# Sums of squares per head in the forgetting attention's projections: two products of fp32r parts in place of one fp32 product

## The reference, cut to what matters

```python
h = rms_norm(x, mix_norm[i])
fq, fk, fv, f_logit, sq, sk, sv, g_fox, g_sb = split_columns(h @ w_in[i])
fq = rms_norm(fq.reshape(b, s_len, FOX_HEADS, HEAD_DIM), q_norm[i])
fk = rms_norm(fk.reshape(b, s_len, FOX_HEADS, HEAD_DIM), k_norm[i])
fv = fv.reshape(b, s_len, FOX_HEADS, HEAD_DIM)
log_f = jax.nn.log_sigmoid((f_logit + forget_bias[i]).astype(jnp.float32))
y_fox = forgetting_attention(fq, fk, fv, log_f)
```

## Time and profile before

| what | us |
|---|---|
| median of three runs | 1746.71 (1746.61 to 1747.81) |
| the profiled execution's own time | 1746.88 |
| its span | 1745.0 |
| PE busy in it | 1724.5 (99%) |
| VectorE busy | 1045.9 (60%) |
| ScalarE busy | 636.7 (36%) |
| POOL busy | 723.5 (41%) |

### The profile page before, as it was taken

The page is one execution under the profiler, slowest core; times in us unless marked ns, Lnnn a source line. Parts: engine busy times, 40 slices in busy tenths (PEclk is TensorE's granted clock), DMA queues, the critical chain, the costliest instruction groups (busy, mean ns, idle before and its releaser), DMA issues.

```text
span 1745.0 us, 21400 instructions
## 1 busy us (share of the span) xinstructions
PE 1724.5 (99%) x7750; PEld 1398.0 (80%) x7750; DVE 1045.9 (60%) x1212; ACT 636.7 (36%) x885; POOL 723.5 (41%) x307
## 2 busy tenths in 40 slices
PE   8999999999999999999999999999999999999999
PEld 6787788887788888888788788887877777888887
DVE  6767367766665456367774457785534753869451
ACT  5222222225655656221322222213445644333321
POOL 2444344443434431344444344444355433444443
PEclk9999999999999999999999999999999999999999
DMA  4332233325211221243333233322342014222243
GB/s 169 112 106 94 82 97 97 107 94 181 85 61 61 92 66 37 80 132 98 123 97 112 82 109 97 102 95 91 113 155 73 25 37 169 89 93 97 97 141 113
DMA packets 44833, 172.63 MB, mean 99 GB/s; under 512 B 5033, under 2 KB 5161, under 8 KB 43980
## 3 DMA queue, kind: packets, MB, share of 16 engines
q1 hardware_dynamic: 39312, 150.23, 26.3%
q10 hardware_dynamic: 5436, 21.20, 3.4%
HBM read 160.79 MB, written 10.62 MB: 98 GB/s over the span
## 4 chain that ended last, share of the span: by engine, by line
issue 52%; PE 31%; POOL 14%; DVE 1%; ACT 1%; POOLq 1%; DMA 0%; SPq 0%; ACTq 0%; DVEq 0%
POOL wlo L268 14%; PE psum L302 9%; PE psum L304 8%; PE psum L303 8%; PE psum L1662 2%; PE psum L1651 1%; DVE Y_lo L2589 0%; PE psum L703 0%; PE psum L688 0%; POOLq L276 0%; DMA raw<-wk_dram 0%; PE psum L674 0%; PE psum L1623 0%; PE psum L675 0%; ACT whi L290 0%
## 5 line engine op out<-in xcount | busy, mean ns | idle before, releaser
L268 POOL TENSOR_TENSOR wlo<-raw,whi 128x1024 fp32r<-128x1024 f32 (+2 forms) x262 | 671.2, 2562 | 931.7 <-ACT whi L290 931.2
L290 ACT ACTIVATE whi<-raw 128x1024 fp32r<-128x1024 f32 (+2 forms) x263 | 290.3, 1104 | 738.0 <-PE psum L304 732.4
L302 PE MATMUL psum<-h_hi,whi 128*128 128x512 f32 x1360 | 538.3, 396 | 4.0 <-POOL wlo L268 2.9
L304 PE MATMUL psum<-h_hi,wlo 128*128 128x512 f32 x1360 | 529.7, 390 | 0.0
L303 PE MATMUL psum<-h_lo,whi 128*128 128x512 f32 x1360 | 529.7, 389 | 0.0
L302 PEld LDWEIGHTS psum<-h_hi,whi 128*128 128x128 f32 x1360 | 255.5, 188 | 63.3 <-issue 5.7
L303 PEld LDWEIGHTS psum<-h_lo,whi 128*128 128x128 f32 x1360 | 255.6, 188 | 54.8 <-issue 3.1
L304 PEld LDWEIGHTS psum<-h_hi,wlo 128*128 128x128 f32 x1360 | 255.4, 188 | 53.8
L302 PE MATMUL psum<-mid_hi,whi 128*128 128x512 f32 x352 | 138.1, 392 | 0.0
L303 PE MATMUL psum<-mid_lo,whi 128*128 128x512 f32 x352 | 137.0, 389 | 0.0
L304 PE MATMUL psum<-mid_hi,wlo 128*128 128x512 f32 x352 | 137.0, 389 | 0.0
(11 more groups left out here) (355 smaller groups left out, 2438.3 us busy)
## 6 DMA issues: line engine op xcount, KB each, us to landing
raw<-wk_dram SPq DMA_DIRECT2D x224, 512.0 KB, 3.7
raw<-wd_dram SPq DMA_DIRECT2D x32, 704.0 KB, 4.1
raw<-wp_dram SPq DMA_DIRECT2D x8, 640.0 KB, 3.8
spectra_scratch<-spec_out ACTq DMA_DIRECT2D x8, 512.0 KB, 7.2
x_scratch<-xT ACTq DMA_DIRECT2D x2, 2048.0 KB, 7.6
xT<-x_scratch ACTq DMA_DIRECT2D x8, 512.0 KB, 4.5
spec<-spectra_scratch ACTq DMA_DIRECT2D x2, 2048.0 KB, 10.3
xT<-x_dram SPq DMA_DIRECT2D x4, 512.0 KB, 7.7
```

Of the source, the lines that this page charges most:

```text
L268: pool.tensor_tensor(wlo[s][:, 0:w], raw[s][:, 0:w], whi[s][:, 0:w].bitcast(F32), ALU.subtract).then_inc(lo_ready, 1)
L290: act.activation(whi[s][:, 0:w], raw[s][:, 0:w], ACT.Copy).then_inc(hi_ready, 1)
L302: pe.matmul(dst, s_hi, m_hi, start=start and i == 0, stop=False, **kw)
L304: last = pe.matmul(dst, s_lo, m_hi, start=False, stop=stop and i == n - 1, **kw)
```

## The change

The square (still made by ScalarE in fp32) is split on VectorE into two fp32r parts, a copy and a subtraction (`vector_square`). The low part overwrites the square, the high part has one buffer of its own. ScalarE makes an fp32r copy of the block of ones once. PE then makes two matmuls for each sum, one of the high part and one of the low part. VectorE's splits stand in its order one round ahead: that of unit 0 behind the constants, that of unit i+1 at the head of round i, before the wait for that round's factor. PE's sum waits for VectorE's split (`made`) in place of ScalarE's square. The semaphore that counted the constants is renamed to `made` and counts the splits too, so the waits on it have other numbers.

```diff
--- before.py
+++ after.py
@@ -155,6 +155,10 @@
         fk_hi = at(72, "fk_hi", [P, HEADS, T], F32R)
         v_pairs = [at(88, "v_pairs0", [P, 2, 2 * T], F32R),
                    nc.alloc_sbuf_tensor_at("v_pairs1", [P, 2, 2 * T], F32R, offset=scratch0)]
+        square_hi = at(88, "square_hi", [P, T], F32R)
+        square_lo = [nc.alloc_sbuf_tensor_at(f"square_lo{i}", [P, T], F32R, offset=scratch0 + (1 - i) * 2048)
+                     for i in range(2)]
+        heads_r = at(90, "heads_r", [P, P], F32R)
         prob = at(96, "prob", [P, TT, T])
         forgets = at(100, "forgets", [P, T], F32R)
         probT = [at(104 + 2 * i, f"probT{i}", [P, T]) for i in range(2)]
@@ -683,7 +687,7 @@
                 if n >= 2:
                     pe.wait_ge(self.lo, n - 1)
                 else:
-                    pe.wait_ge(foxp.cleared, n + 10)
+                    pe.wait_ge(foxp.made, n + 26)
                 for t in range(s, TT):
                     last = pe.transpose(psum[:, 512 * (4 + s % 2) + t * P:512 * (4 + s % 2) + (t + 1) * P],
                                         self.prob[h % 2][:, t, s * P:(s + 1) * P], ident)
@@ -696,7 +700,7 @@
                         pe.wait_ge(self.out, h)
                         pe.wait_ge(self.out_hi, 2 * h)
                     else:
-                        pe.wait_ge(foxp.cleared, 12)
+                        pe.wait_ge(foxp.made, 28)
                         pe.wait_ge(merge1.seven_read, 1)
                 both = v_pairs[s // 2][:, s % 2, h * P:(h + 1) * P]
                 for i, part in enumerate((probT_hi, probT_lo)):
@@ -706,7 +710,7 @@
 
             def tensor(self, pe):
                 pe.wait_ge(constr_ready, 1)
-                pe.wait_ge(foxp.cleared, 9)
+                pe.wait_ge(foxp.made, 25)
                 pe.wait_ge(foxp.ready, 32)
                 pe.wait_ge(foxp.forget, 11)
                 pe.wait_ge(foxp.softplus, 7)
@@ -855,9 +859,9 @@
 
 
             def __init__(self):
-                (self.sq, self.sum, self.std, self.rstd, self.f32, self.hi, self.ready, self.cleared, self.forget,
+                (self.sq, self.sum, self.std, self.rstd, self.f32, self.hi, self.ready, self.made, self.forget,
                  self.softplus, self.v) = (
-                    sem(f"fox_{x}") for x in ("square", "head_sum", "std", "rstd", "f32", "hi", "qk_ready", "constants",
+                    sem(f"fox_{x}") for x in ("square", "head_sum", "std", "rstd", "f32", "hi", "qk_ready", "made",
                                               "forget", "softplus", "v"))
 
             def unit(self, j):
@@ -893,10 +897,14 @@
                         linear_by_token(pe, (7, 6, 4, 5), BASE["fox_v"] + j, j, 4, h_hi, h_lo)
 
             def tensor_square_sum(self, pe, i):
-                pe.wait_ge(self.sq, i + 1)
+                if i == 0:
+                    pe.wait_ge(constr_ready, 2)
+                pe.wait_ge(self.made, 2 * i + 11)
                 if i >= 2:
                     pe.wait_ge(self.std, i - 1)
-                pe.matmul(bank(4 + i % 2), block_ones, head_sq[i % 2][:, :], start=True, stop=True).then_inc(self.sum, 1)
+                pe.matmul(bank(4 + i % 2), heads_r[:, :], square_hi[:, :], start=True, stop=False)
+                pe.matmul(bank(4 + i % 2), heads_r[:, :], square_lo[i % 2][:, :], start=False,
+                          stop=True).then_inc(self.sum, 1)
 
             def scalar(self, act):
                 act.wait_ge(const_landed, 32)
@@ -909,6 +917,8 @@
                         if j >= 2:
                             act.wait_ge(self.sum, j - 1)
                         act.activation(head_sq[j % 2][:, :], bank(j % 4), ACT.Square).then_inc(self.sq, 1)
+                        if j == 0:
+                            act.activation(heads_r[:, :], block_ones, ACT.Copy).then_inc(constr_ready, 1)
                         split_hi_to(act, u + 3)
                     if j == 0:
                         for m in range(1, 4):
@@ -958,12 +968,15 @@
                     rows = other[h % 2]
                     row = vec[rows, VEC["head_row"] + h:VEC["head_row"] + h + 1]
                     dve.tensor_scalar(fq_hi[rows, h, :], any_finite[rows, :], 0.0, row, ALU.mult,
-                                      ALU.add).then_inc(self.cleared, 1)
-                dve.tensor_scalar(small[:, 31:32], col("q_norm"), HD ** -0.5, None, ALU.mult).then_inc(self.cleared, 1)
+                                      ALU.add).then_inc(self.made, 1)
+                dve.tensor_scalar(small[:, 31:32], col("q_norm"), HD ** -0.5, None, ALU.mult).then_inc(self.made, 1)
+                self.vector_square(dve, 0)
                 for i in range(8):
+                    if i < 7:
+                        self.vector_square(dve, i + 1)
                     dve.wait_ge(self.rstd, i + 1)
                     if i == 0:
-                        dve.wait_ge(self.cleared, 9)
+                        dve.wait_ge(self.made, 13)
                     if i == 1:
                         dve.wait_ge(filters.stored, 64)
                     gain = small[:, 31:32] if i < 4 else col("k_norm")
@@ -998,7 +1011,7 @@
                 for i, (t, b) in list(enumerate(((0, 7), (2, 4), (3, 5), (1, 6))))[first:last]:
                     dve.wait_ge(self.v, i + 1)
                     dve.tensor_tensor(self.value_part(t, 1), self.heads(bank(b)), self.value_part(t, 0).bitcast(F32),
-                                      ALU.subtract).then_inc(merge1.seven_read if b == 7 else self.cleared, 1)
+                                      ALU.subtract).then_inc(merge1.seven_read if b == 7 else self.made, 1)
 
             def heads(self, b):
                 return b.rearrange("p (a e c) -> p a e c", e=2, c=HD)
@@ -1006,6 +1019,17 @@
             def value_part(self, t, lo):
                 v = v_pairs[t // 2][:, t % 2, :].rearrange("p (a e c) -> p a e c", e=4, c=HD)
                 return v[:, :, 1:3, :] if lo else v[:, :, 0:4:3, :]
+
+            def vector_square(self, dve, i):
+                square32 = head_sq[i % 2][:, :]
+                dve.wait_ge(self.sq, i + 1)
+                dve.wait_ge(unit_done, self.unit(i) + 1)
+                if i:
+                    dve.wait_ge(self.sum, i)
+                dve.tensor_copy(square_hi[:, :], square32).then_inc(self.made, 1)
+                dve.wait_ge(self.made, 2 * i + 10)
+                dve.tensor_tensor(square_lo[i % 2][:, :], square32, square_hi[:, :].bitcast(F32),
+                                  ALU.subtract).then_inc(self.made, 1)
 
             def vector_logits(self, dve):
                 dve.wait_ge(unit_done, BASE["fox_f"] + 1)
```

## The result

The changed kernel takes 1759.29 us (median of 4, 1757.68 to 1760.76) against 1746.85 before: ratio 1.0068 (1.0056 to 1.008), **slower by 12.4 us**. The profiled execution took 1757.68, at the lower end of the four, and 10.8 more than the profiled one of the kernel before.

What follows compares the result with a forecast made beforehand. PE's queue was taken to set the end: waits of 15.3 us less 3.3 saved give +12.0, so 1746.7 becomes 1758.7 us, range 1749.7 to 1764.5. This chain of waits, with the first port race won, had chance 0.47.

Steps and rivals of the forecast that it cites:

- (a) The first sum: Before sum 0: VectorE's first split stands behind the constants, so PE waits till 419.2, 2.75 us.
- The port race: VectorE's first subtraction (418.45) before POOL's op (418.56); POOL first would make the wait 5.1, total 1761.0, chance 0.2.
- The end of unit 3: POOL's op at 438.45 precedes VectorE's copy by 0.4 us; STT (L971) is 2.4 late, and the loop starts.
- The waits: PE waits 1.25 for unit 6's split, 2.3, 3.2, 4.65 before sums 5 to 7, 0.95 for the bank behind.
- The last term: Behind the last sum, the unit after next waits 0.2 us longer for its split.
- The clock: Half rate behind PE's longest pause would cost 0 to 1.7 us, taken as 0; rival with one or two ramps: 0.12.
- The saving: On PE, a sum costs 0.46 in place of 0.87 us: 8 x 0.41 = 3.3 us gained.
- Rival 3: VectorE's copy beats POOL's op at unit 3's end, so only (a) is paid: -0.6 us, 1746.1, chance 0.15.

Runs made afterwards that it cites:

- first experiment: Changed kernel with VectorE's first split moved ahead of the eight constants, nothing else changed: 1755.21 us, ratio 1.0047 to the kernel before.
- the run with one product: Changed kernel without low part and VectorE's splits: 1749.41 us. With softplus, VectorE's gate work and last logarithm moved too (the three moves): 1744.59 us.

## Why the prediction was right, and where it was not

The mechanism came out: VectorE's splits close a loop with ScalarE and POOL, and PE waits. The time did too (1758.7 forecast, 1759.29 measured), but that the two are 0.6 us apart is in part luck. In the traced execution the waits are 11.9 where 15.3 was forecast, 1.5 went to the clock and 0.5 to slow second intervals where 0 was, and it grew by 10.8, not 12.4. By its steps:

- **(a) The first sum.** 2.75 forecast, 2.56 found. The port race was less close than 0.1 us: the copy starts at 418.25, before the recorded end of the op ahead of it (418.19 and 0.14), so the subtraction stood at 418.70 against POOL's 419.13.
- **The end of unit 3.** "The copy is held till 441.1": held to 441.53. L971 was forecast for 441.97 and stood at 442.17, in an execution that was 0.5 late from the start.
- **The waits** 1.25, 2.3, 3.2, 4.65, 0.95 became 1.13, 1.98, 2.72, 2.73, 0.74. The last big one is smaller because 1.5 us of PE's time went to the clock just ahead of it, inside the same cover; 2.73 + 1.5 is 4.2. The first experiment bears this out: there half rate lay ahead of sum 6, whose wait was 1.09, and the wait before sum 7 was 4.27. The last term, 0.2 for the unit after next, was nothing: PE waited 0.48 there, as before.
- **The clock.** "I take 0, since it is nearer to 1.44" is the step that failed. A pause of 2.72 was followed by half rate and one of 2.73 in the same execution was not, and in the first experiment 1.96 was enough. The size, forecast as at most 1.7, was 1.5. How much of it shows in the time while VectorE sets the pace no run parts. The Trainium skill (TensorE: Matmul & The Clock Gate, HAM oscillation) describes such a return to half rate behind a pause; these rows agree, the printed clock of 0.50 too. That the executions at 1760.6 and 1760.8, with a lower mean clock (0.996 against 0.998 and 0.999), hold one or more further ramps is likely and not shown, since only the one at 1757.68 has a trace.
- **The saving.** 3.3 forecast, 0.41 a sum. Two sums without a pause between them are 5.89 apart (430.99 to 436.88), before 6.35: 0.46 a sum, 3.7 in eight, and 13.4 + 0.5 of losses less 10.3 of growth leaves 3.6. By the run without the saving it went for the most part into wider waits.
- **Rival 3, "the loop doesn't close"**, was priced on a wrong door. It asked only whether VectorE's copy comes ahead of POOL's op at the end of unit 3. It closed as well in the runs with a split held there by only 0.4 us and with no split at all, through ScalarE: "squares unit 4 at 445.9" was in my walk, as a consequence of the held split, but the softplus lump with a shorter unit is enough. Its -0.6 could not have come out by that point alone. It also had no wait at the last sum: with POOL's ops narrow, 2.2 before that sum and 0.74 behind it stayed, so the price was too low by 2.9.

What stays open: whether the 0.85 us for the gate unit's low part can be had back too; moving that copy of weights ahead was not tried. Open too are which of the three moves keeps the loop open in the run with one product, and what parts the two groups of its executions.

## What to carry to other kernels

Before a bound engine is made faster, look at how far the others are from colliding: here 0.68 us off each unit, with no work added on VectorE, was enough to close a loop of VectorE, ScalarE and POOL that costs more than the saving. A wait on the engine that feeds such a loop (ScalarE's 0.83 us for the unit) is not waste but the distance that keeps POOL's op off VectorE's pairs. Spread lumps, put short work where an engine waits anyway, and count an op on VectorE that can meet POOL's 2.4 us op at that much more: a copy of 0.43 took up to 2.60 here, a subtraction of 0.69 up to 2.86.

## What the runs showed of the hardware

POOL gets in between two VectorE ops that stand back to back: 3.00 us for a pair of copies with a price of 0.87, in each late round. The Trainium skill (SBUF — State Buffer, Who interferes with whom) says that VectorE and GpSimd share a pair of ports, and that of a VectorE op that uses both its pairs and an op of GpSimd whichever issues first gets the shared pair for the whole instruction; the rows agree (the held copy of 439.13 ends 0.29 behind POOL's op), and add that a queue of VectorE ops does not keep the ports.

PE's clock can fall to half rate behind a pause of 2 us, but the length of the pause alone does not tell. Behind pauses of 1.96, 2.58 to 2.59 (in three runs), 2.72, 3.85, 3.87, 4.25 and 4.27 it fell; behind 1.98, 2.12, 2.25, 2.56, 2.73 and 3.23 it did not. In the run with one product it fell behind 1.26 and 1.43 with a single matmul between them.
